# State space part by token tiles of 128: one decay matrix per head over both chunks of a tile

## The chip, the cores and the metric

The kernel runs on one core of a Trainium2 chip, in one launch. The metric is the device time of a run in microseconds; of the kernel before three runs are shown. The profile is of one more execution. Engines are named as in the profile: PE is TensorE's matmul, PEld its weight load, DVE is VectorE, ACT ScalarE, POOL GpSimd, SP SyncE, which issues the loads.

## The reference, cut to what matters

A first block (16 meta tokens and 256 tokens, width 1024) has a mixer of two branches, gated linear attention and a state space part, and then a retrieval feed-forward with 16384 experts; a second block has retention and stick-breaking attention. The change is in the state space part alone (32 heads of 64 columns in 4 groups of 8; state 128). The reference walks it in chunks of 64 tokens:

```python
def ssd_chunk_step(S, inp):
    xdt, a, Bc, Cc = inp
    acum = jnp.cumsum(a, axis=1)
    seg = jnp.exp(-jnp.abs(acum[:, :, None] - acum[:, None, :]))
    cb = jnp.einsum('btgn,bsgn->btsg', Cc, Bc)
    y = jnp.einsum('btsgr,btsg,bsgrp->btgrp', seg, cb, xdt)
    y = y + jnp.einsum('btgn,bgrpn,btgr->btgrp', Cc, S, jnp.exp(acum))
    to_end = jnp.exp(acum[:, -1:] - acum)
    S = S * jnp.exp(acum[:, -1])[..., None, None] + jnp.einsum('bsgn,bsgr,bsgrp->bgrpn', Bc, to_end, xdt)
    return S, y
```

Inside a chunk every token sees every other one, earlier and later, by `exp(-|difference of the sums|)`; across chunks it sees earlier ones only, through the state S. y then gets `d_skip * x`, is multiplied by silu(z), normed in groups of 512 and goes through `w_up_ssd`.

## The kernel before, in words

**Stream.** All weights come as 512 KB chunks ("units", loaded by SP into four buffers `raw`). `do_split` (L202) makes of each a high part on ACT (`whi`, L208) and a low part on DVE (`wlo`, L209), four units ahead of their use (`AHEAD`), and PE makes three passes per product (L247). `stream_T` (L256) takes a unit of 128 output columns over 1024 rows: 8 x 3 = 24 passes with 256 or 272 tokens moving. `stream_N` (L282) takes a unit of 512 columns over 256 rows: two halves of 6 passes with 512 columns moving.

**Side work.** Everything else is written as generators in the list `sides`. While `ring["steps"]` is 2, `side_step` (L232) runs one piece of the first generator in the middle of a unit and one at its end; a generator that ends uses up a step too. `until(key)` (L696) runs steps at once until a result has been issued. The order so made is each engine's program order: every engine takes its instructions in that order and waits at semaphores. ACT and DVE instructions other than the splits are chained one behind another.

**Order around the change.** 8 units for B and C (convolved by `conv`, L675, on ACT and DVE: L679, L681, L683, and the silu L673 one unit later), 16 units for gates, 16 units for x (four per group of heads), 8 units for the product of the attention branch (L845), 16 units of z (`stream_N`; `use_z` L854 with the product L860 and the square L861), then 16 units over the 2048 features of y. `first_side` (L727) turns B and calls `decays(0)` during the gates. `ssd_side(g)` (L736) is appended when the fourth x unit of group g is used; `conv_x` (L828) forces `xsg{g-2}`, the turned x of the group whose buffer it takes. `y_side(g)` (L872) is appended after z block g: `rstd` (L329, small DVE instructions around one square root on ACT), `diagonals` (L319, L321 and L322), some empty steps, then transposes of y by `turned` (L324, products at L306) and splits (L316, L317). `y_side(3)` has its first piece issued at the end of z, before what is left in `sides`.

**The state space part.** In the gate part (L494 to L525) the running sums of `a` are made per chunk by a scan with resets, exps of them, one decay factor per chunk and head broadcast through PE (`dec`), and the sums go to DRAM (`scr`). `load_bc(g)` (L810) fetches them back as 4 transfers of 128 KB, each row broadcast to 64 partitions. `decays(g)` (L701) makes M: C.B products of 64x64 into one bank (L711), two subtractions (L714), `min(m, -m)` (L718), exp (L719), two products with C.B out of PSUM (L722); M is [128 tokens, tile, head, 64 tokens]. `ssd_side` turns x and makes XD, the skip part of Y (`turn`, L751, L754) and XE (`to_end`, L760), makes the state of the 16 meta tokens (L772, L773), and then for each of two tiles and two chunks: eight products M x XD of 64x64 for the 8 heads, the state read C x S (512 columns moving), and but for the last chunk the update B x XE and `S = S*dec + update` (L790, L793). `next(ahead)` runs a piece of `decays(g + 1)` in between. After each tile Y takes in the bank (L797), then the state part (L799, L802). Buffers: `bank_free[4]` to `[6]` for y, state read and update; `bank_free[7]` for C.B.

An fp32 product (`mm`, L306; transposes L309) shows as two passes in the trace.

## Time and profile before

| | us |
|---|---|
| runs: median, lowest, highest | 1656.56, 1653.85, 1658.47 |
| the profiled execution | 1659.78 |
| its span, from first to last instruction | 1658.0 |
| PE, DVE, ACT busy in it | 1440.6, 1103.1, 700.5 |

### The profile page before, as it was taken

To read this page: it belongs to the slowest core of one execution; us is meant where nothing else is said; L and a number is where in the kernel's file an instruction comes from. 1 tells how busy PE (TensorE), PEld (TensorE's weight loads), DVE (VectorE), ACT (ScalarE), POOL (GpSimd) and SP (SyncE) were. 2 spreads that over 40 slices of the span, in tenths; PEclk is the share of its full clock that TensorE was granted. 3 is DMA by queue.
4 is the path that set the end of the run, shared out by engine and by line. 5 is a ranking of instruction groups with operands and counts; after the bars stand their busy time and mean duration, and the time that the engine had idled before them with its cause. 6 is when DMAs were issued, how large, how long until landed. Compare 5 with 4: busy or idle time off the path is not lost. (4 is left out here: it accounts for less than half of the span.)

```text
span 1658.0 us, 19318 instructions
## 1 busy us (share of the span) xinstructions
PE 1440.6 (87%) x6761; PEld 1007.9 (61%) x6761; DVE 1103.1 (67%) x2091; ACT 700.5 (42%) x1196; POOL 300.1 (18%) x260
## 2 busy tenths in 40 slices
PE   6999898999899699878777877877799999799987
PEld 6987696776798534333333333333288688788866
DVE  5765468786667868777777777675577466645554
ACT  5664465434545332222222222221354465666853
POOL 0000000000001356445435444433100000000000
PEclk9999999999999889898989899989899999899999
DMA  6452253243464999999999999999845456454432
GB/s 219 145 163 80 87 169 98 89 141 103 152 217 163 419 414 421 422 421 421 422 421 422 421 421 422 420 421 407 305 134 178 135 178 196 127 160 140 153 118 85
DMA packets 78000, 415.64 MB, mean 251 GB/s; under 512 B 9024, under 2 KB 9024, under 8 KB 44880
## 3 DMA queue, kind: packets, MB, share of 16 engines
q0 software_dynamic: 36864, 268.45, 39.1%
q1 hardware_dynamic: 41040, 145.96, 27.8%
q8 instruction: 54, 0.88, 0.2%
q14 instruction: 42, 0.34, 0.1%
HBM read 413.29 MB, written 1.08 MB: 250 GB/s over the span
## 5 line engine op out<-in xcount | busy, mean ns | idle before, releaser
L306 PE MATMUL ps<-AR 128*128 128x512 f32 (+7 forms) x1368 | 413.7, 450 | 111.9 <-ACT AR L1167 76.1
L209 DVE TENSOR_TENSOR wlo<-raw,whi 128x1024 fp32r<-128x1024 f32 x257 | 312.1, 1222 | 176.6 <-ACT whi L208 174.5
L306 PEld LDWEIGHTS ps<-AR 128*128 128x128 f32 (+3 forms) x1368 | 201.7, 185 | 303.8 <-issue 150.7
L208 ACT ACTIVATE whi<-raw 128x1024 fp32r<-128x1024 f32 x257 | 269.7, 1054 | 131.4 <-PE ps L247 116.5
L247 PE MATMUL ps<-XH,whi 128*128 128x256 f32 (+1 forms) x1032 | 306.1, 297 | 6.3 <-DVE XL L317 4.5
L306 PE MATMUL ps<-SLAB,AR 128*128 128x512 f32 x516 | 252.3, 645 | 59.6 <-ACT AR L1167 59.0
L247 PE MATMUL ps<-XL,whi 128*128 128x256 f32 (+1 forms) x1032 | 297.3, 288 | 0.0
L247 PE MATMUL ps<-XH,wlo 128*128 128x256 f32 (+1 forms) x1032 | 297.1, 288 | 0.0
L1132 POOL DMA_INDIRECT AR<-in_peer_uv,C x127 | 149.8, 1180 | 710.7 <-PE ps L247 528.4
L306 PEld LDWEIGHTS ps<-SLAB,AR 128*128 128x128 f32 x516 | 104.3, 207 | 205.9 <-issue 123.2
L247 PEld LDWEIGHTS ps<-XH,whi 128*128 128x128 f32 x1032 | 200.9, 195 | 26.2 <-issue 14.9
L247 PEld LDWEIGHTS ps<-XL,whi 128*128 128x128 f32 x1032 | 200.7, 194 | 0.1
L247 PEld LDWEIGHTS ps<-XH,wlo 128*128 128x128 f32 x1032 | 200.4, 194 | 0.0
L1141 DVE CUSTOM_DVE_ANT_0 SLAB<-SLAB,AR 128x1024 f32<-128x1024 f32 x129 | 156.6, 1222 | 64.2 <-DMA SLAB<-in_peer_uv,C 64.2
L247 PE MATMUL ps<-whi,XH 128*128 128x512 f32 x480 | 196.6, 409 | 0.0
L1141 DVE CUSTOM_DVE_ANT_0 AR<-AR 128x1024 f32<-128x1024 f32 x127 | 154.2, 1223 | 55.9 <-DMA AR<-in_peer_uv,C 55.8
L247 PE MATMUL ps<-whi,XL 128*128 128x512 f32 x480 | 188.2, 392 | 0.0
L247 PE MATMUL ps<-wlo,XH 128*128 128x512 f32 x480 | 188.0, 392 | 0.0
L1132 POOL DMA_INDIRECT SLAB<-in_peer_uv,C x129 | 150.1, 1164 | 169.8 <-PE ps L306 132.5
L1167 ACT ACTIVATE AR<-C 128x128 f32<-128x128 f32 x254 | 84.1, 392 | 186.6 <-DVE C L1155 156.3
L1150 ACT ACTIVATE C<-C,SM 128x4 f32<-128x4 f32 (+2 forms) x68 | 20.2, 297 | 293.7 <-DVE C L1141 293.4
L247 PEld LDWEIGHTS ps<-whi,XH 128*128 128x128 f32 x480 | 90.7, 189 | 23.3 <-issue 5.6
(228 smaller groups left out, 1175.0 us busy)
## 6 DMA issues: line engine op xcount, KB each, us to landing
raw<-in_stream SPq DMA_DIRECT2D x257, 512.0 KB
SLAB<-in_peer_uv,C POOLq DMA_INDIRECT x129, 27.5
AR<-scr SPq DMA_DIRECT2D x16, 128.0 KB, 3.9
AR<-in_rows SPq DMA_DIRECT2D x4, 512.0 KB, 4.7
AR<-in_peer_uv,C POOLq DMA_INDIRECT x127, 27.1
AR<-in_con SPq DMA_DIRECT2D x1, 1280.0 KB, 5.4
AR<-in_xin SPq DMA_DIRECT2D x2, 512.0 KB, 5.1
AR<-in_xin SPq DMA_DIRECT2D x1, 1024.0 KB, 5.8
```

What stands on the lines that cost most here:

```text
L208: a = A(lambda e: e.activation(h[:, :], r, ACT.Copy), loaded[i], free, chain=False)
L209: b = V(lambda e: e.tensor_tensor(l[:, :], r, h[:, :].bitcast(F32), ALU.subtract), a, loaded[i], free, chain=False)
L247: tok = PE(lambda e, s=s, m=m, n=n: e.matmul(out_ap, s, m, start=first and n == 0, stop=last and n == 2), *(after if n == 0 else ()), sign ...
L306: return PE(lambda e: e.matmul(out_ap, l, r, start=start, stop=stop, skip_group_check=onto), *after, signal=sig)
L1132: G(lambda e: e.indirect_dma_start(slots[j], None, peer_uv, bass.IndirectOffsetOnAxis(ap=col, axis=0)).then_inc(s, 16), idx_pt[m // 16], f ...
L1141: dot_pt[m] = V(lambda e: e.tensor_tensor_reduce(u, u, HN[:, i, :], 1.0, 0.0, ALU.mult, ALU.add, AV[:, i, at:at + 1]), uv_in[m], chain=False)
L1150: gelu_pt[ms[0]] = A(lambda e: e.activation(CC[:, i, c], AV[:, i, c], ACT.Gelu_apprx_tanh, scale=SM[:, 24 + i:25 + i]), dot_pt[ms[-1]])
L1167: a = A(lambda e: e.activation(d, ident, ACT.Copy, scale=CC[:, i, c]), c_ready, dg_free.get(m - 4), chain=False)
```

## The change

The running sums are taken over tiles of 128 tokens (resets at tokens 0, 16 and 144), with one decay factor, at the border between the two tiles; M becomes [128 tokens, tile, head, 128 tokens] and also carries the part from the first chunk of a tile to its second, with C.B copied by ACT to a masked SBUF tile CBM whose lower left quarter stays zero. The state is read twice per group and updated once. The pieces of `decays` go from 5 to 7, those of `ssd_side` from 16 to 15, and 13 for the last group (by the count of `yield`). DY moves, as M is twice as long.

```diff
...
@@ gate part
-            v = V(lambda e: e.tensor_tensor_scan(STK[W, :], C1[W, C_SCAN:C_SCAN + T], dx, 0.0, ALU.mult, ALU.add))
+            V(lambda e: e.memset(dq, 1.0))
+            for at in (0, 16, 144):
+                V(lambda e, at=at: e.memset(dq[:, at:at + 1], 0.0))
+            v = V(lambda e: e.tensor_tensor_scan(STK[W, :], dq, dx, 0.0, ALU.mult, ALU.add))
...
-            for c in range(4):
-                at = 16 + 64 * c + 63
-                v = V(lambda e, c=c, at=at: e.tensor_scalar(SM[W, 32 + 32 * c:64 + 32 * c], C1[W, C_ID:C_ID + 32],
-                                                            dq[:, at:at + 1], None, ALU.mult), c_ready)
+            v = V(lambda e: e.tensor_scalar(SM[W, 32:64], C1[W, C_ID:C_ID + 32], dq[:, 143:144], None, ALU.mult), c_ready)
-            tok = mm(ps[4][:, 0:128], SM[W, 160:288], SM[W, 32:160], True, True, True, v, v1, bank_free[4])
-            bank_free[4] = pts["dec"] = V(lambda e: e.tensor_copy(SM[:, 288:416], ps[4][:, 0:128]), tok)
+            tok = mm(ps[4][:, 0:32], SM[W, 160:288], SM[W, 32:64], True, True, True, v, v1, bank_free[4])
+            bank_free[4] = pts["dec"] = V(lambda e: e.tensor_copy(SM[:, 288:320], ps[4][:, 0:32]), tok)
...
@@ buffers
-        XE = place("XE", 18384, 1536).rearrange("p (i c) -> p i c", i=3)
-        M = place("M", 2768, 2048).rearrange("p (b i r t) -> p b i r t", b=2, i=2, r=8)
+        XE = place("XE", 18384, 1024).rearrange("p (i c) -> p i c", i=2)
+        CBM = place("CBM", 19408, 512).rearrange("p (b i t) -> p b i t", b=2, i=2)
+        M = place("M", 2768, 4096).rearrange("p (b i r t) -> p b i r t", b=2, i=2, r=8)
...
@@ decays(g)
             for i in range(2):
-                for c in range(2):
-                    cols = slice(16 + 128 * i + 64 * c, 16 + 128 * i + 64 * c + 64)
-                    tok = mm(ps[7][64 * c:64 * c + 64, 64 * i:64 * i + 64], BT[:, g, cols], CT[:, g, cols], True, True,
-                             i == 1 and c == 1, bank_free[7], [pts[f"c{f}"] for f in (16 + g, 20 + g)])
-            cb = tok
+                cols = slice(16 + 128 * i, 144 + 128 * i)
+                tok = mm(ps[7][:, 128 * i:128 * i + 128], BT[:, g, cols], CT[:, g, cols], True, True, i == 1, bank_free[7],
+                         [pts[f"c{f}"] for f in (16 + g, 20 + g)])
+            cbm = CBM[:, g % 2, :, :]
+            two = ps[7][:, 0:256].rearrange("p (i t) -> p i t", i=2)
+            A(lambda e: e.copy(cbm[0:64, :, :], two[0:64, :, :]), tok, cbm_zero, pts.get(f"M{g - 2}"))
+            cb = bank_free[7] = A(lambda e: e.copy(cbm[64:128, :, 64:128], two[64:128, :, 64:128]))
             for i in range(2):
                 v = V(lambda e, i=i: e.tensor_tensor(
-                    Mg[:, i, :, :], Mg[:, i, :, :], STN[:, i, 8 * g:8 * g + 8].unsqueeze(2).broadcast_to([128, 8, 64]),
+                    Mg[:, i, :, :], Mg[:, i, :, :], STN[:, i, 8 * g:8 * g + 8].unsqueeze(2).broadcast_to([128, 8, 128]),
                     ALU.subtract), pts[f"bc{g}"])
-            yield
-            v = V(lambda e: e.scalar_tensor_tensor(Mg, Mg, -1.0, Mg, ALU.mult, ALU.min))
-            a = A(lambda e: e.activation(Mg, Mg, ACT.Exp), v)
-            yield
+                yield
+            for i in range(2):
+                v = V(lambda e, i=i: e.scalar_tensor_tensor(Mg[:, i, :, :], Mg[:, i, :, :], -1.0, Mg[:, i, :, :], ALU.mult, ALU.min))
+                a = A(lambda e, i=i: e.activation(Mg[:, i, :, :], Mg[:, i, :, :], ACT.Exp), v)
+                yield
             for i in range(2):
...
+                    Mg[:, i, :, :], Mg[:, i, :, :], cbm[:, i, :].unsqueeze(1).broadcast_to([128, 8, 128]), ALU.mult), a, cb)
-            pts[f"M{g}"] = bank_free[7] = v
+            pts[f"M{g}"] = v
...
@@ first_side()
+            nonlocal cbm_zero
+            cbm_zero = V(lambda e: e.memset(CBM[:, :, :, :], 0.0), pts["ox"])
...
@@ ssd_side(g)
             to_end(0)
             yield
-            to_end(1)
-            yield
             for i in range(2):
-                for c in range(2):
-                    rows_ = slice(64 * c, 64 * c + 64)
...
+                cols = slice(16 + 128 * i, 144 + 128 * i)
+                tok = mm(ps[5][:, :], CT[:, g, cols], SS[:, :], True, True, True, s_ready, bank_free[5])
+                if i == 0:
+                    u = mm(ps[6][:, :], BN[:, 0, 128 * g:128 * g + 128], XE[:, 0, :], True, True, True, bank_free[6], xe[0])
+                    k = 288 + 8 * g
+                    V(lambda e: e.tensor_tensor(
+                        SS.rearrange("p (r c) -> p r c", r=8), SS.rearrange("p (r c) -> p r c", r=8),
+                        SM[:, k:k + 8].unsqueeze(2).broadcast_to([128, 8, 64]), ALU.mult), u, pts["dec"])
+                    s_ready = bank_free[6] = V(lambda e: e.tensor_tensor(SS[:, :], SS[:, :], ps[6][:, :], ALU.add))
+                for r in range(8):
+                    tok = mm(ps[4][:, 64 * r:64 * r + 64], Mg[:, i, r, :], XD[:, i, 64 * r:64 * r + 64], True, True, r == 7,
+                             m_ready, xd[i], bank_free[4])
+                pts["pe_ssd"] = tok
+                next(ahead, None)
+                yield
...
@@ load_bc(g)
+            for i in range(2):
+                src = scr[i, 8 * g:8 * g + 8, :].rearrange("r t -> (r t)").unsqueeze(0).broadcast_to([128, 1024])
+                pts[f"bc{g}"] = dma(SP, M[:, g % 2, i, :, :].rearrange("p r t -> p (r t)"), src, s_bc[g % 2], pts["scr"],
                                     pts["ox"], pts.get("pe_ssd"))
...
-        DY = place("DY", 4816, 512).rearrange("p (b i c) -> p b i c", b=2, i=2)
+        DY = place("DY", 0, 512).rearrange("p (b i c) -> p b i c", b=2, i=2)
...
```

## Rows read from the trace of the kernel before

**Rows 1.** The page: busy time of each engine; GB/s in 40 slices of the span.

```profile
PE 1440.6 (87%) x6761; PEld 1007.9 (61%) x6761; DVE 1103.1 (67%) x2091; ACT 700.5 (42%) x1196; POOL 300.1 (18%) x260
...
GB/s 219 145 163 80 87 169 98 89 141 103 152 217 163 419 414 421 422 421 421 422 421 422 421 421 422 420 421 407 305 134 178 135 178 196 127 160 140 153 118 85
```

**Rows 2.** By stretch: length, busy of PE, PEld, DVE, ACT, POOL; clock, DMA share, GB/s.

```profile
239.90:290.80 50.90, 43.29 (x308) 34.94 (x306) 42.81 (x63) 25.18 (x40) 0.00 (x0) 0.97 0.36 107
290.80:334.00 43.20, 41.97 (x292) 33.65 (x292) 32.15 (x46) 16.65 (x22) 0.00 (x0) 0.92 0.28 89
334.00:355.00 21.00, 20.08 (x144) 13.90 (x142) 18.05 (x26) 4.95 (x5) 0.00 (x0) 1.00 0.52 165
355.00:396.00 41.00, 40.87 (x213) 27.04 (x212) 31.14 (x38) 17.33 (x24) 0.00 (x0) 1.00 0.33 104
396.00:423.90 27.90, 26.11 (x134) 21.72 (x134) 18.48 (x35) 18.90 (x27) 0.00 (x0) 1.00 0.47 137
423.90:437.00 13.10, 8.42 (x56) 7.82 (x55) 8.02 (x23) 8.05 (x15) 0.00 (x0) 0.89 0.47 168
```

**Rows 3.** Timeline of PE, x stream: start, length, line, operands, passes, idle before.

```profile
251.45 0.29 PE L247 MATMUL ps<-XH,whi 128*128 128x272 f32 x1
251.58 0.29 PE L247 MATMUL ps<-XL,whi 128*128 128x272 f32 x1
...
254.19 3.20 PE L306 MATMUL ps<-AR 64*64 64x64 f32 x20
...
265.37 0.45 PE L306 MATMUL ps<-AR 128*64 128x64 f32 x8
...
267.45 1.14 PE L306 MATMUL ps<-AR 64*64 64x64 f32 x16
268.86 2.12 PE L306 MATMUL ps<-AR 128*64 128x512 f32 x4 [0.27 <-DVE AR L799]
...
272.63 2.21 PE L306 MATMUL ps<-AR 64*64 64x64 f32 x18
...
283.95 1.74 PE L309 MATMUL ps<-C,AR 128*128 128x128 f32 x12
```

**Rows 4.** Groups by line and shape, 200 to 560 us: count, busy us, mean ns, idle before.

```profile
L306 PEld LDWEIGHTS ps<-AR 64*64 64x64 f32 x256 | 16.1, 134 | 3.4 <-issue 1.4 <-DVE wlo L209 0.4 <-DVE AR L754 0.4
L306 PEld LDWEIGHTS ps<-AR 128*128 128x128 f32 x120 | 15.6, 197 | 8.7 <-DVE AR L322 6.8 <-ACT AR L1026 1.7
...
L790 DVE TENSOR_TENSOR AR<-AR,SM 128x512 f32<-128x512 f32 x12 | 8.3, 692 | 9.3 <-PE ps L306 8.8
...
L679 ACT COPY AR<-ps 128x272 f32<-128x272 f32 x16 | 6.2, 387 | 24.3 <-PE ps L247 23.6
...
L714 DVE TENSOR_TENSOR AR<-AR 128x512 f32<-128x512 f32 x8 | 5.5, 692 | 5.4 <-DMA AR<-scr 4.9
...
L718 DVE SCALAR_TENSOR_TENSOR AR<-AR 128x1024 f32<-128x1024 f32 x4 | 4.9, 1225 | 0.1
...
L719 ACT ACTIVATE AR<-AR 128x1024 f32<-128x1024 f32 x4 | 4.2, 1059 | 23.8 <-DVE AR L718 23.8
```

**Rows 5.** The transfers from scr, 205 to 360 us: issue ns, time to landing.

```profile
L188 SPq DMA_DIRECT2D AR<-scr x16: 451/596/937, 210.4 to 344.8; - x16
...
DMA to landing us min/median/max: 2.7/3.9/5.3
```

**Rows 6.** Waits, 239.9 to 290.8 us: us in total, times, longest.

```profile
DVE AR L683 <- ACT AR L681: 4.9, 4, 2.2
```

**Rows 7.** Timeline of PE behind the forced transposes.

```profile
290.78 2.07 PE L306 MATMUL ps<-AR 16*128 16x512 f32 x2 [5.10 <-DVE AR L760]
```

**Rows 8.** Timeline of PE where y is turned.

```profile
418.02 1.16 PE L306 MATMUL ps<-AR 128*128 128x128 f32 x8 [1.79 <-DVE AR L322]
...
433.79 1.77 PE L306 MATMUL ps<-AR 128*128 128x128 f32 x8 [4.33 <-DVE AR L322]
```

**Rows 9.** Timeline of DVE after the z stream.

```profile
430.24 0.29 DVE L322 TENSOR_SCALAR AR<-C,SM 128x128 f32<-128x128 f32 x1
```

More of the change, by code:

```diff
@@ L157, in build @@
         ps = [ctx.enter_context(nc.psum_tensor(f"ps{i}", [128, 512], F32)) for i in range(8)]
-        scr = nc.dram_tensor("scr", [4, 32, 64], F32).ap()
+        scr = nc.dram_tensor("scr", [2, 32, 128], F32).ap()
         PE = Engine(sem("s_pe"), False)
@@ L523, in gates_side @@
             s_scr = sem("s_scr")
-            pts["scr"] = dma(SP, scr.rearrange("c r t -> r c t"), STK[W, 16:T].rearrange("p (c t) -> p c t", c=4), s_scr,
+            pts["scr"] = dma(SP, scr.rearrange("i r t -> r i t"), STK[W, 16:T].rearrange("p (i t) -> p i t", i=2), s_scr,
                              pts["stk"])
@@ L664, in build @@
         xp_free = [None, None]
+        cbm_zero = None
         v0 = V(lambda e: e.memset(XP[:, :, 0:3], 0.0), x_ready)
@@ L759, in to_end @@
             def to_end(i):
-                xe[i] = V(lambda e: e.tensor_tensor(heads(XE[:, i, :]), heads(XD[:, i, :]), each(STN[:, i, 32 + 8 * g:40 + 8 * g]),
+                xe[i] = V(lambda e: e.tensor_tensor(heads(XE[:, i // 2, :]), heads(XD[:, i, :]), each(STN[:, i, 32 + 8 * g:40 + 8 * g]),
                                                     ALU.mult))
@@ L775, in ssd_side @@
             yield
-            to_end(1)
-            yield
             for i in range(2):
-                for c in range(2):
-                    rows_ = slice(64 * c, 64 * c + 64)
-                    cols = slice(16 + 128 * i + 64 * c, 16 + 128 * i + 64 * c + 64)
-                    for r in range(8):
-                        mm(ps[4][rows_, 64 * r:64 * r + 64], Mg[rows_, i, r, :], XD[rows_, i, 64 * r:64 * r + 64], True, True,
-                           False, m_ready, xd[i], bank_free[4])
-                    tok = mm(ps[5][rows_, :], CT[:, g, cols], SS[:, :], True, True, True, s_ready, bank_free[5])
-                    pts["pe_ssd"] = tok
-                    if not (i == 1 and c == 1):
-                        u = mm(ps[6][:, :], BN[rows_, i, 128 * g:128 * g + 128], XE[rows_, i, :], True, True, True, bank_free[6], xe[i])
-                        k = 288 + 32 * (2 * i + c) + 8 * g
-                        V(lambda e, k=k: e.tensor_tensor(
-                            SS.rearrange("p (r c) -> p r c", r=8), SS.rearrange("p (r c) -> p r c", r=8),
-                            SM[:, k:k + 8].unsqueeze(2).broadcast_to([128, 8, 64]), ALU.mult), u, pts["dec"])
-                        s_ready = bank_free[6] = V(lambda e: e.tensor_tensor(SS[:, :], SS[:, :], ps[6][:, :], ALU.add))
-                    next(ahead, None)
-                    yield
@@ L811, in load_bc @@
             until("ox")
-            for c in range(4):
-                i, rows_ = c // 2, slice(64 * (c % 2), 64 * (c % 2) + 64)
-                src = scr[c, 8 * g:8 * g + 8, :].rearrange("r t -> (r t)").unsqueeze(0).broadcast_to([64, 512])
-                pts[f"bc{g}"] = dma(SP, M[rows_, g % 2, i, :, :].rearrange("p r t -> p (r t)"), src, s_bc[g % 2], pts["scr"],
+            for i in range(2):
+                src = scr[i, 8 * g:8 * g + 8, :].rearrange("r t -> (r t)").unsqueeze(0).broadcast_to([128, 1024])
+                pts[f"bc{g}"] = dma(SP, M[:, g % 2, i, :, :].rearrange("p r t -> p (r t)"), src, s_bc[g % 2], pts["scr"],
                                     pts["ox"], pts.get("pe_ssd"))
```

10 lines of the change are left out of this document (4 added, 6 removed).

## The prediction

> **What bounds the kernel now.** The page comes first: one execution of 1658.0 us in which PE is busy 87%, DVE 67%, ACT 42% [rows 1]. Those are averages, so the view by stretches comes next, cut where the state space work begins and ends [rows 2]. From 239.9 to 423.9 us PE is busy in 172.3 of 184.1 us (43.29 + 41.97 + 20.08 + 40.87 + 26.11), DVE in 142.6. PE is the bound, but in the first stretch DVE has 42.8 of 50.9 us, 84%: take work from PE there and DVE is next. The timeline of PE then shows what the side work costs [rows 3], and the same view further on, with the groups of instructions by line, where PE stands and for whom.
>
> The order of everything is fixed by the program: two side steps per streamed unit (a unit is 24 passes; two starts in [rows 3], at 251.45 and 251.58, are 0.126 apart, so 3.03 us). I number steps by units of the 16 that make x: ssd_side(0) starts at 4.0; now it takes 16 steps per group (the last one only ends it), so the second is at 12.0 when the use of unit 12 forces three steps at 13.0. y_side(0) follows ssd_side(3) at 34.5, y_side(1) at 37.5, y_side(2) at 40.5; the z stream ends at 40.0.
>
> **PE work of a group, before.** A step for one chunk holds 16 passes 64x64 (8 products, two passes each), two passes of the state read and two of the update: 3.20 us, twice in this group, and once in two pieces, 1.14 + 2.12; the last chunk has no update, 2.21 [rows 3]. Sum 11.87 us, of which the modelled tails are about 0.2: 11.7. The C.B products are 8 short passes, 0.45 us [rows 3], and 4 full ones after: nothing.
>
> **After.** Two state reads and one update: 3 x 1.06 (2.12 for two products, [rows 3]) = 3.2 us; 64 or 128 contracted rows don't show in those times. The 16 passes of a tile now have 128x128 weights and still 64 moving columns, a form that no row has. Below: the 64x64 passes, 1.14 us for 16. Above: 12 transposes with 128x128 weights and 128 columns took 1.74 [rows 3], so 16 would take 2.3. The weight loads are nearest: 134 ns for 64 columns, 197 for 128, so 63 ns more per 64 columns [rows 4]; if loading bounds the pass it grows from 58 (1.14 less a 0.22 tail, by 16) to about 110 ns. I take 110 ns, 1.8 us per tile, and keep 1.14 and 2.3. Per group 3.2 + 3.6 = 6.8 against 11.7: 4.9 us saved, ends 3.9 and 6.2; four groups 19.6, ends 15.6 and 25.
>
> The Trainium skill (TensorE: Matmul & The Clock Gate, section LDWEIGHTS) gives a load P/1.2 ns for P columns whatever the rows, so 53 ns becomes 107 and the fewer, fuller products hardly gain in this part. The 63 ns per 64 columns agrees; by the page's figure the saving would be 5.1 us a group in place of 4.9.
>
> **DVE and ACT.** Durations from [rows 4]. Per group the decays cost DVE now 4 instructions of 512 elements (0.692) and one of 1024 (1.225) = 3.99; after, 6 of 1024: 7.35, so +3.36. Gone: one to_end (0.692) and two of three state updates (2 x 2 x 0.692): -3.46. Net -0.1: DVE does not get lighter. Its waits for the update products (8.8 us in 8, [rows 4]) shrink, since there is one update instead of three and it is issued ahead of the 16 passes. ACT gets one more exp (1.06) and two copies (0.39 for 272 columns, so at most 0.8): +1.9 on an engine that is half idle. No silu falls between the two exps of groups 1 to 3, so no table load (1.28) is added. The four memsets and three fewer tensor_scalars in the gate part, the 512-column memset of CBM and the narrower dec copy lie in the streams before 239.9 us, inside the four units by which splits lead: nothing, bounds -1 and +1 us.
>
> **DMA.** 4 x 128 KB become 2 x 512 KB per group; issue to landing is 3.9 us median, 5.3 worst [rows 5]. SP issues two where it issued four, behind the same wait for PE, with the raw loads queued behind them: not worse. The extra 512 KB at 422 GB/s, the most in a slice [rows 1], is 1.2 us, at half that 2.5. DVE waited for this transfer once, 4.9 us [rows 4], in the gate stream, where PE had no gap; it will be 6 to 8 us, inside the four units (12 us) that splits run ahead. The other groups give it three side steps (4.5 us or more) as now. What is queued behind the waiting subtraction is wlo, then PE. Cost nothing, worst +3.
>
> **Step counts.** After, an ssd_side takes 15 steps (the last group 13). Three consequences.
> (a) Stretch 239.9 to 290.8, up to the forced step: PE stands 5.10 us for L760 behind the forced transposes [rows 7]. PE saves 4.9 here, but DVE's own order up to that L760 is unchanged at 42.8 us of work; the 8.1 us it is idle are mostly the wait for ACT's L681 (4.9, [rows 6]) and small gaps. I let DVE reach 90% (42.8/0.9 = 47.5): gain 3.4 us, floor 0, ceiling 5.6 (DVE gapless but for 2.5 us). PE waits longer at 285.69, not less, and the half clock behind it stays (0.92 over 43.2 us in [rows 2], so 3.5 us lost).
> (b) 290.8 to 396: three groups, 14.7 us. DVE has 81.3 of 105.2 us; 81.3/90.5 is 90%, again at that edge. I take 13, floor 5.
> (c) 423.9 on: z ends with y_side(3) and then y_side(2) issuing their rstd; PE stands 4.33 us up to 433.79 for the second L322 [rows 8], and the clock of the stretch is 0.89 [rows 2], 1.4 us lost. After, y_side(0) starts at 32.0, (1) at 35.0, (2) at 38.0, so (2) has its diagonals ready two units before PE wants them, at 41.5. Gone: 4.3 + 1.4 = 5.7. Late next is y_side(3), whose diagonals end at 430.5 [rows 9], 6.6 us after the z stream (423.9), as now, and are wanted at 44.0, 12 us after: covered. On the other hand y_side(0) now starts right behind the square of its block, as (3) does: 6.6 us from the last z pass to L322, against three steps of 6 passes with 512 columns (0.126 x 512/272 x 6 = 1.4 us each, an estimate), 4.2 of cover: a gap of 2.4, where y_side(1)'s gap of 1.79 at 418.02 [rows 8] goes. With a chance of half-rate time behind it I count -1.
>
> Sum 3.4 + 13 + 5.7 - 1 = 21 us. The profiled execution took 1659.78 (1658.0 of span, 1.8 around it), 3.2 above the median 1656.56; against the median: 1635.5.
>
> **Rivals.**
> 1. VectorE is the bound throughout. For it: 84% and 86% (18.05 of 21.0) in two stretches, and the two engines meet at each group (PE waits for L799 at 268.86 in [rows 3], for L760 in [rows 7]). Against: 76% in 290.8 to 396 and 41 us of it at PE 100%. Then (b) gives its floor of 5 and (a) 1.5: with 5.7 - 1 that is 11, less 3.5 for one more spell of half rate like the one in (a): 8, so 1648.5.
> 2. The weights load free and the passes stay at 58 ns: 1.3 us a group more (5 in all), 1630.5. For it: loads run beside the passes in every stream (PEld 61% busy, PE 87%); against: the 12 transposes in 1.74.
> 3. The stall at the z end stays (the change does not shift it as I count, or DVE's order brings another wait): 6 less, 1641.5. For it: the diagonals come out of a chain of small instructions between DVE and ACT with splits in between [rows 9], where a new wait is easily made; against: three groups give half a unit each and one more.
> 4. Slower. One mechanism: each exp sits in ACT's queue until DVE has made its operand, and the whi splits queue behind it. Now 23.8 us in 4, 5.95 each [rows 4]. Two per group hold ACT 2 x (5.95 + 1.06) = 14.0 us, against the 12.1 us of lookahead; with the 5.1 us DVE is behind PE at the forced step, PE stands 14.0 - 12.1 + 5.1 = 7.0 us and pays 1.7 for half rate (half of the 3.5 above): 8.7 in each of groups 1 to 3, 26 in all, 5 above the gain: 1661. It decides from a hold of 12 us. Against it: the two exps are a step apart, the second's operand is made while the first waits, and in 355 to 396, which holds the last exp, PE is busy 40.87 of 41.0 us.
>
> **Chances.** Forecast 0.42; rival 1 0.22; rival 2 0.15; rival 3 0.14; rival 4 0.07. 0.3% is 5 us, what can be told from no change. Rival 1 leaves 0.03 within it and rival 4 0.01; slower 0.06, same 0.04, faster 0.90. Range 1624 (cheap passes, all of DVE's idle time used) to 1649 (rival 1).
>
> **What would show it.** The 64-column passes near 1.8 us for 16; L306 busy down by some 20 us; DVE above 88% in the x stretch, with a longer PE wait for to_end behind the forced transposes; no gap before the L306 transposes after the z stream; bc transfers landing within 6 us. Wrong if PE's gaps grow by as much as its work shrinks, or if DVE's sum in these stretches changes by more than 2 us.

## The result and the profile after

The changed kernel takes 1669.46 us (median of 7 runs, 1662.78 to 1675.78) against 1656.56 for the kernel before in the same comparison; ratio 1.0075, 95% interval 1.0052 to 1.0098. It is slower by 0.75%, some 13 us. The prediction said 1635.5, range 1624 to 1649, with 0.06 for slower: wrong in sign, by 34 us. The profiled execution of after is its slowest run, 1675.78 us (span 1673.9), so its trace shows more of the loss (15.9 us of span) than the median does.

The page after, busy time of each engine and the group of the side products (answers to [rows 1]):

```profile
PE 1430.0 (85%) x6585; PEld 1014.4 (61%) x6585; DVE 1102.3 (66%) x2077; ACT 703.3 (42%) x1206; POOL 300.4 (18%) x260
...
L306 PE MATMUL ps<-AR 128*128 128x512 f32 (+8 forms) x1192 | 398.0, 485 | 132.6 <-ACT AR L1168 79.8
```

PE did 10.6 us less, although more of it ran at half rate. DVE's sum moved by 0.8. So the work is as forecast; the time went elsewhere. By stretches, with the columns of [rows 2] (the borders are set by the waits of this trace and don't lie at the same work as there):

```profile
226.40:242.30 15.90, 12.38 (x97) 12.15 (x96) 13.45 (x18) 14.46 (x21) 0.00 (x0) 1.00 0.52 169
242.30:290.10 47.80, 41.17 (x260) 37.74 (x260) 33.73 (x48) 19.72 (x33) 0.00 (x0) 0.86 0.34 109
290.10:303.30 13.20, 0.04 (x1) 0.05 (x1) 10.41 (x14) 8.41 (x13) 0.00 (x0) 0.61 0.31 88
303.30:343.50 40.20, 37.85 (x236) 33.68 (x236) 27.53 (x37) 16.79 (x24) 0.00 (x0) 0.83 0.29 91
343.50:382.00 38.50, 33.55 (x188) 27.16 (x188) 30.06 (x37) 10.32 (x13) 0.00 (x0) 0.91 0.42 135
382.00:412.00 30.00, 23.70 (x81) 16.45 (x81) 18.63 (x23) 8.21 (x13) 0.00 (x0) 0.72 0.34 105
```

The third line is the picture of the case: 13.2 us in which PE does nothing and DVE is busy for 10.41. In [rows 7] the same wait was 5.10. The timeline of PE after, with the columns of [rows 3]:

```profile
259.22 2.86 PE L306 MATMUL ps<-AR 128*128 128x512 f32 x18 [0.52 <-DVE AR L766]
...
268.58 5.81 PE L306 MATMUL ps<-AR 128*128 128x512 f32 x22 [1.91 <-DVE AR L801]
...
303.25 2.07 PE L306 MATMUL ps<-AR 16*128 16x512 f32 x2 [13.18 <-DVE AR L766]
...
420.60 1.16 PE L306 MATMUL ps<-AR 128*128 128x128 f32 x8 [2.24 <-DVE AR L322]
```

(L766 is the `to_end` that was L760, L801 the emptying of bank 5 that was L799, L306 the product line of both.) The waits view of after, 205 to 425 us, shows who stood for whom: line, releaser, us in total, times, longest.

```profile
ACT AR L724 <- DVE AR L723: 26.5, 8, 5.8
...
PE ps L306 <- DVE AR L766: 22.2, 4, 13.2
...
ACT AR L715 <- PE ps L306: 16.7, 3, 6.8
DVE AR L685 <- ACT AR L683: 15.7, 6, 6.0
...
DVE AR L718 <- DMA AR<-scr: 6.0, 1, 6.0
...
PE ps L306 <- DVE AR L801: 4.7, 3, 2.3
...
PE ps L309 <- ACT AR L675: 4.2, 1, 4.2
...
PE ps L247 <- ACT AR L694: 3.5, 1, 3.5
```

The same view of the kernel before, PE alone:

```profile
PE ps L306 <- DVE AR L760: 6.0, 2, 5.1
PE ps L309 <- ACT AR L673: 2.2, 1, 2.2
PE ps L306 <- DVE AR L322: 1.8, 1, 1.8
PE ps L306 <- DVE AR L799: 0.9, 2, 0.6
```

To compare kernels I line them up by the low splits (L209, one per unit, the same work in the same order everywhere). "Split 44" is in the gates, 52 near the end of the gates, 64 near unit 12 of x, 84 in z, 100 behind z. Worked out from the traces, between the starts of splits 44 and 100:

```
                     wall   PE gaps  lost to half rate  the rest
before               261.5    17.6         8.5           235.4
after                276.6    41.4        25.0           210.2
start of split       52     64     84     96     100   (after less before, us)
                    +3.8  +12.5  +25.0  +15.4  +13.6

                            (a) split 52 to the meta-state  (b) from there   (c) split 84
                            product of group 1              to split 84      to 100
before                      62.5                            96.8             71.6
after                       71.1                           109.3             60.3
e3  read in bank 6          64.7                           100.5             61.2
e13 and 14 steps            60.8                            97.0             57.8
e14 as e8, 15 steps         62.3                           101.0             61.9
e10 before, less PE work    61.2                            89.4             70.3
```

(The last four kernels are told of below.) The borders hold the same units of the stream, but not the same side work: in before the last two chunks of group 3 (32 of the 64-column passes) come behind split 84, in after all of group 3 comes ahead of it. So (b) of after holds a little more side work, and (c) less.

"PE gaps" are idle times over 0.25 us (shorter ones count in "the rest"); "lost to half rate" is half of the time outside gaps in which the records show a granted clock of 1.2 GHz in place of 2.4. PE's work fell by 25.2 us, and gaps (+23.8) and half rate (+16.5) gave back 40. The experiments ask what made the gaps.

### The profile page after: what moved, and what is told of

It is laid out like the page before. It is cut to its first block and busy times, and to the rows that moved or that the text cites. A ratio compares the mean times of both kernels' runs of the same rounds, so it can differ in the third digit from the quotient of the medians.

```text
span 1673.9 us, 18970 instructions
## 1 busy us (share of the span) xinstructions
PE 1430.0 (85%) x6585; PEld 1014.4 (61%) x6585; DVE 1102.3 (66%) x2077; ACT 703.3 (42%) x1206; POOL 300.4 (18%) x260
## 5 line engine op out<-in xcount | busy, mean ns | idle before, releaser
L306 PE MATMUL ps<-AR 128*128 128x512 f32 (+8 forms) x1192 | 398.0, 485 | 132.6 <-ACT AR L1168 79.8
L209 DVE TENSOR_TENSOR wlo<-raw,whi 128x1024 fp32r<-128x1024 f32 x257 | 311.5, 1221 | 183.5 <-ACT whi L208 181.4
L306 PEld LDWEIGHTS ps<-AR 128*128 128x128 f32 (+4 forms) x1192 | 203.5, 205 | 317.2 <-issue 145.3
L247 PE MATMUL ps<-XH,whi 128*128 128x256 f32 (+1 forms) x1032 | 307.6, 298 | 9.7 <-DVE XL L317 5.1
L306 PE MATMUL ps<-SLAB,AR 128*128 128x512 f32 x516 | 253.3, 646 | 61.8 <-ACT AR L1168 61.0
L247 PE MATMUL ps<-XL,whi 128*128 128x256 f32 (+1 forms) x1032 | 299.1, 290 | 0.0
L247 PE MATMUL ps<-XH,wlo 128*128 128x256 f32 (+1 forms) x1032 | 298.9, 290 | 0.0
L306 PEld LDWEIGHTS ps<-SLAB,AR 128*128 128x128 f32 x516 | 104.0, 206 | 208.7 <-issue 122.6
L247 PEld LDWEIGHTS ps<-XH,whi 128*128 128x128 f32 x1032 | 202.8, 197 | 22.5 <-DVE XL L317 8.1
L247 PEld LDWEIGHTS ps<-XL,whi 128*128 128x128 f32 x1032 | 202.8, 196 | 0.1
L247 PEld LDWEIGHTS ps<-XH,wlo 128*128 128x128 f32 x1032 | 202.5, 196 | 0.0
L247 PE MATMUL ps<-whi,XH 128*128 128x512 f32 x480 | 197.2, 411 | 0.0
L247 PE MATMUL ps<-whi,XL 128*128 128x512 f32 x480 | 189.1, 394 | 0.0
L247 PE MATMUL ps<-wlo,XH 128*128 128x512 f32 x480 | 188.9, 394 | 0.0
L247 PEld LDWEIGHTS ps<-whi,XH 128*128 128x128 f32 x480 | 91.4, 190 | 19.8 <-issue 2.5
```

The lines of the kernel that those rows point to most:

```text
L209: b = V(lambda e: e.tensor_tensor(l[:, :], r, h[:, :].bitcast(F32), ALU.subtract), a, loaded[i], free, chain=False)
L247: tok = PE(lambda e, s=s, m=m, n=n: e.matmul(out_ap, s, m, start=first and n == 0, stop=last and n == 2), *(after if n == 0 else ()), sign ...
L306: return PE(lambda e: e.matmul(out_ap, l, r, start=start, stop=stop, skip_group_check=onto), *after, signal=sig)
```

## Experiments

All were compared over 5 rounds with the kernel before on the same chip (its medians 1656.2 to 1659.1), so ratios can be set side by side. 0.001 is 1.66 us. Stretches, gaps and waits are read from the one profiled execution of each.

### Is it ScalarE's new copies?

**e1_cb_late**: the changed kernel, the two copies of C.B behind the second exp.

```diff
-            A(lambda e: e.copy(cbm[0:64, :, :], two[0:64, :, :]), tok, ...)      # before the subtractions
-            cb = bank_free[7] = A(lambda e: e.copy(cbm[64:128, :, 64:128], ...))
+                if i == 1: (the same two, behind the exp of tile 1)
```

> The changed kernel, with the two ACT copies of C.B issued behind the second exp (two and a half side steps later); nothing else moved. Theory A (the copies hold ACT's queue for PE, 16.7 us in three groups, the x convolution behind them waits, and DVE idles 6.0 us in front of L685 for it): the wait in front of the copies falls below 2 us, DVE's idle in front of the convolution halves, the 13.2 us gap of PE behind the forced transposes falls to 6 to 8, and the time falls from 1669 to about 1657 (1652 to 1662). Theory B (DVE's pieces are too large and bunched, the copies only stand where ACT would wait for the convolution's input anyway): less than 4 us, 1665 to 1669.

Measured 1672.36, ratio 1.0100 [1.0083, 1.0118]: nothing won against after (1.0075 [1.0052, 1.0098]).

**e2_before_cbcopy**: the kernel before, with such copies added.

```diff
-            cb = tok
+            A(lambda e: e.copy(cbm[:, 0:64], ps[7][:, 0:64]), tok, ...)
+            cb = bank_free[7] = A(lambda e: e.copy(cbm[:, 64:128], ps[7][:, 64:128]))
```

> The kernel before, with C.B copied by ACT from PSUM to SBUF (two copies of 128x64 per group, at the place where the change has them) and the product taken from there. Theory A: ACT waits here for PE too, so some 5 to 10 us slower than before, 1662 to 1667, with DVE idle in front of the convolution. Theory B: within 2 us of before, 1655 to 1659.

Measured 1657.74, ratio 1.0012 [1.0002, 1.0022]. The copies cost next to nothing where they are added and nothing is won where they are moved: they are not the cause. The 6.8 us for which L715 waits in after is ACT waiting for PE, which itself waits.

### The second state read and bank 5

**e3_bank6**: the changed kernel; the state read of tile 1 goes to bank 6 (free by then), so that it doesn't wait until L801 has emptied bank 5.

```diff
-                tok = mm(ps[5][:, :], CT[:, g, cols], SS[:, :], ..., bank_free[5])
+                rb = 5 + i
+                tok = mm(ps[rb][:, :], CT[:, g, cols], SS[:, :], ..., bank_free[rb])
```

> The changed kernel, with the second state read of a group going to the bank of the update (free once the update is added, for which the read waits anyway) in place of the bank that L801 must empty. Theory C (the second tile is issued one step behind L801, so PE stands for DVE, 4.7 us in three, half clock follows, and what waits behind it, the copies of C.B on ACT above all, waits with it): the L801 waits vanish, C.B comes earlier and the time falls by 5 to 10 us, to 1660 to 1665. Theory A alone, or B: 1 to 3 us less, as PE waits for M or the drained y bank instead.

Measured 1658.04, ratio 1.0017 [1.0001, 1.0033]: 0.0058 less than after, 9.6 us. The same question from the other side:

**e7_extra_step**: the changed kernel, bank 5 kept, with one empty step between L801 and the second read.

```diff
                 pts[f"y{g}{i}"] = V(... yg, yg, IN ...)
                 next(ahead, None)
                 yield
+                if i == 0:
+                    yield
```

> The changed kernel (second read in the bank that L801 empties, as it was) with one more empty side step between L801 and the second read, so 16 steps per group again. If the short distance from L801 to the read is what cost 11 us (shown so far only by using another bank), the L801 waits shrink from 4.7 us in three to under 2 and the time falls by 6 to 10 us, to 1659 to 1663, though the z end loses its advantage of a step. If the other bank helped for another reason, 1667 or more.

Measured 1663.87, ratio 1.0049 [1.0035, 1.0064]: 0.0026 less than after, with intervals that overlap. The L801 waits shrink from 4.7 us in 3 to 1.2 in 2, and stretch (b) falls from 109.3 to 96.0 us, while (c) grows from 60.3 to 66.4, as more steps lie behind split 84. So it supports e3, in the stretch where the wait was, but as a whole it is not clear of noise. In after one tile's read, emptying and next read lie so close that the second read waits for L801, and in program order behind it stand the C.B products, behind these ACT's L715, behind this the conv copies and DVE's L685: the waits of L801, L715 and L685 above. That this chain is what makes 2 us into 10 is argued from the order; e1, where L715 stood elsewhere, shows that it is not needed in just this form (there PE waited 3.6 us for the exp in its place). In the kernel before more steps lay between, and the wait was 0.9 us in 2.

### What the step count does

**e4_before15**: the kernel before, `to_end(1)` in the step of `to_end(0)`: 15 steps instead of 16.

```diff
             to_end(0)
-            yield
             to_end(1)
```

> The kernel before, with the second to_end in the piece of the first, so that each group takes 15 side steps and not 16; the same instructions. By the prediction's step (c) y_side(2) has its diagonals ready before z ends: PE's 4.33 us wait for L322 and the half rate behind it go, 1656.6 falls to about 1651 (1649 to 1654), and no wait comes in x. Rival: fewer steps crowd DVE in the x stream and give the same back: 1655 to 1660.

Measured 1657.20, ratio 1.0023 [1.0002, 1.0044]. The stall of 4.33 us behind z [rows 8] is gone as forecast in (c), but 6.9 us of shift there had been built up before it by other waits and half rate: stretch (b) takes 106.0 us in place of 96.8, (c) 64.8 in place of 71.6, and nothing is won.

**e8_bank6_oneexp**: e3 with one min and one exp over both tiles, and so one step fewer, 14.

```diff
-            for i in range(2):
-                v = V(... Mg[:, i, :, :] ... ALU.min)
-                a = A(... Mg[:, i, :, :] ... Exp, v)
-                yield
+            v = V(... Mg ... ALU.min)
+            a = A(... Mg ... Exp, v)
+            yield
```

> The kernel with the second read in the update's bank, with one scalar_tensor_tensor and one exp over both tiles of M (2048 elements) in place of two each, in one step: the same elements, two instructions and one step less per group. If two exps per group in ACT's queue are what holds the convolution and the splits (rival 4 of the prediction), ACT's wait for DVE falls and the time by 3 to 6 us, to 1652 to 1655. If the holding is by the bunching of DVE's work, the longer pair holds ACT longer at a time: same or 1 to 4 us slower, 1657 to 1662.

Measured 1647.89, ratio 0.9950 [0.9930, 0.9970]: 11 us less than e3. Two things were changed at once, so they were then taken apart.

**e13_twoexp_14steps**: e3 with both min/exp pairs kept, but in one step.

```diff
                 a = A(lambda e, i=i: e.activation(Mg[:, i, :, :], Mg[:, i, :, :], ACT.Exp), v)
-                yield
+            yield
```

> The changed kernel with the second state read in bank 6 (1658.0 us, ratio 1.0017 with 15 steps per group), with both halves' min and exponential kept as two instructions each but issued in one step of work instead of two: 14 steps. The one-exponential kernel (0.9950) differed from it in both. If the step fewer made its 10 us: ratio 0.994 to 0.997. If the second exponential in ScalarE's queue made them: 1.000 to 1.003.

Measured 1646.45, ratio **0.9943 [0.9927, 0.9958]**.

**e14_oneexp_15steps**: e8 with an empty step behind the exp (`+ yield`).

> The one-exponential kernel (1647.9 us, 0.9950, 14 steps) with one empty step behind the exponential: 15 steps as in the changed kernel. The other half of the same question: if the step count is what counts, 1.000 to 1.003; if the number of exponentials is, 0.994 to 0.997.

Measured 1655.17, ratio 0.9992 [0.9978, 1.0005]. With 14 steps two exps are as good as one (0.9943, 0.9950); with 15 both lose 7 to 12 us. It is the step, not the second exp in ScalarE's queue (the two kernels with 15 steps are 4 us apart, with intervals that just overlap). (In the kernel before, one step fewer gained nothing, e4: what a step is worth belongs to the order around it.) Waits of PE, 200 to 430 us, in e13 and then in e14:

```profile
PE ps L306 <- DVE AR L766: 19.3, 5, 10.0
PE ps L309 <- ACT AR L675: 4.2, 1, 4.2
PE ps L247 <- ACT AR L694: 1.0, 1, 1.0
PE ps L306 <- DVE AR L322: 0.6, 1, 0.6
```

```profile
PE ps L306 <- DVE AR L766: 21.3, 4, 11.7
PE ps L309 <- ACT AR L675: 3.9, 1, 3.9
PE ps L306 <- ACT AR L779: 3.2, 1, 3.2
PE ps L306 <- DVE AR L322: 2.3, 1, 2.3
```

The step more shows only late: at split 64 the two kernels are level (+1.5 and +1.8 against before), at 84 they stand at +0.6 and +6.0, at 96 at -11.6 and -2.0. It brings back a wait for the copy of the meta state in the last group, one for y's diagonals, and 2 us of the wait for `to_end`.

**e17_after_14steps**: the changed kernel with that one `yield` removed and bank 5 kept.

> The changed kernel with nothing altered but the yield between the two min/exponential pairs: both pairs in one step of work, 14 steps per group instead of 15; the second state read still waits in bank 5. With that read in bank 6 the same edit was worth 0.0074 (1.0017 to 0.9943). If the two losses (the read's wait, the 15th step) are separate, they add up: ratio 0.999 to 1.002. If they are one loss seen twice: 1.005 or above (nothing left to win here), or 0.996 and below (the step alone takes both away).

Measured 1660.30, ratio 1.0017 [1.0005, 1.0029]: 0.0058 less than after. The two losses add up: 0.0075 - 0.0058 (bank) - 0.0058 (step) = 0.9959 would be the plain sum, 0.9943 was measured for both.

**e18_twoexp_13steps**: e13 with the two subtractions in one step as well (one `yield` fewer again).

> The second state read in bank 6, both min/exponential pairs in one step (1646.5 us, 0.9943 with 14 steps) and both subtractions of the decays in one step too, as in the kernel before: 13 steps. If each step less goes on paying: 0.988 to 0.991. If 14 steps already bring the groups in ahead of the gated stream and what is left is VectorE's backlog at the forced transposes: 0.993 to 0.996, with the 10 us gap in its place.

Measured 1652.19, ratio 0.9969 [0.9951, 0.9987]: 4 us worse than 14 steps, with intervals that just overlap; e16 below, also with 13 steps, points the same way. Stretch (a) gets shorter still (59.0 us), (b) longer (104.0 against 97.0). Fewer steps are not always better. Its longest wait for `to_end` is 8.3 instead of 10.0 us, but L766 takes 20.4 us in 6 in place of 19.3 in 5.

**e5_bank6_spread0**: e3 with two empty steps in `decays(0)` only, for the 3.5 us that PE waits in the gates (L247 for L694: a bank held by a sigmoid queued behind the exps).

> The kernel with the second read in the update's bank (1658.0), and in the decays of group 0 alone two more empty steps between the transfers of the sums and the first subtraction. Theory D (in the gate stream DVE stands 6 us for the larger transfer, the six wide instructions and two exps bunch behind it, and the sigmoids behind the second exp in ACT's queue hold a bank that PE wants: 3.8 us, then 2.7 behind it in front of the first transposes): both waits shrink to under 1 us, DVE's wait for the transfer to under 2, and the time falls by 4 to 6 us, to 1652 to 1654. Rival: the same work lands two steps later on the x convolution and PE waits there: 1656 to 1660.

Measured 1658.19, ratio 1.0011 [0.9998, 1.0025], e3 had 1.0017. The 3.8 us gap in the gates went, and the next one, ahead of the transposes, grew from 2.7 to 5.9 us.

### VectorE's share

**e6_bank6_halfm**: e3 with M's subtraction, min, exp and product done for heads 0 to 3 of each group only; heads 4 to 7 use M as loaded.

```diff
-                    Mg[:, i, :, :], Mg[:, i, :, :], STN[:, i, 8 * g:8 * g + 8]...broadcast_to([128, 8, 128]),
+                    Mg[:, i, 0:4, :], Mg[:, i, 0:4, :], STN[:, i, 8 * g:8 * g + 4]...broadcast_to([128, 4, 128]),
```

> The kernel with the second read in the update's bank, with subtraction, min, exp and product of M done for heads 0 to 3 of each group only; the other half of M is used as it was loaded. DVE loses 3.7 us and ACT 1.06 per group, PE nothing, step counts stay. If VectorE's work is what takes the place of PE's (rival 1 of the prediction), the 13.2 us gap behind the forced transposes falls by the 3.7 to 5 us and the time by 10 to 16 us, to 1642 to 1648. If it is the order of waits between ACT, DVE and PE, and not the amount, 2 to 6 us: 1652 to 1656.

Measured 1647.31, ratio 0.9946 [0.9930, 0.9962]: 12 us less than e3 for 14.7 us less of DVE work (half of 24 instructions of 1.225 us); ScalarE's exps are halved with it, some 4 us, so the two are not told apart. The wait behind the forced transposes falls from 13.2 to 9.7 us. By stretches (a) falls from 64.7 to 62.3 us, (b) from 100.5 to 93.4: in the changed kernel less VectorE work is worth most in (b).

**e15_oneexp_pool**: e8 with the eight subtractions on GpSimd.

```diff
-                v = V(lambda e, i=i: e.tensor_tensor(Mg[:, i, :, :], ..., ALU.subtract), pts[f"bc{g}"])
+                gs = G(lambda e, i=i: e.tensor_tensor(Mg[:, i, :, :], ..., ALU.subtract), pts[f"bc{g}"], V.now())
```

> The one-exponential kernel with the eight 128x1024 subtractions of the decays (1.22 us each on VectorE) on GpSimd, which does nothing else in this stretch. Theory (what TensorE still waits for is VectorE's backlog: 47.9 us of work between split 52 and split 64, 56.7 us of wall time, the same in five kernels with 46 to 54 us of TensorE work): that stretch falls below 54, the 10.6 us gap below 6, ratio 0.989 to 0.993. Rival (the exponential then waits for the slower subtraction, or the two engines hinder each other): 0.995 or above.

Measured 1651.67, ratio 0.9975 [0.9965, 0.9986]: 4 us worse than e8 (0.9950 [0.9930, 0.9970]), at the edge of noise. Timeline of GpSimd and VectorE in e15 (start, length, line, operands, count, idle before):

```profile
274.48 1.90 POOL L718 TENSOR_TENSOR AR<-AR 128x1024 f32<-128x1024 f32 x1 [4.95 <-DVE AR L804]
274.51 3.25 DVE L685 SCALAR_TENSOR_TENSOR AR<-AR,PAR 128x272 f32<-128x272 f32 x3
...
312.14 1.90 POOL L718 TENSOR_TENSOR AR<-AR 128x1024 f32<-128x1024 f32 x1 [35.76 <-DVE AR L685]
312.23 2.90 DVE L209 TENSOR_TENSOR wlo<-raw,whi 128x1024 fp32r<-128x1024 f32 x1 [0.22 <-ACT whi L208]
...
319.39 1.23 DVE L209 TENSOR_TENSOR wlo<-raw,whi 128x1024 fp32r<-128x1024 f32 x1
319.47 2.90 POOL L718 TENSOR_TENSOR AR<-AR 128x1024 f32<-128x1024 f32 x1 [5.43 <-DVE AR L804]
```

Three L685 that take 1.57 us elsewhere take 3.25, a split that takes 1.22 takes 2.90, each while GpSimd's 1.90 us instruction runs; where VectorE was first, GpSimd's took 2.90. In these rows the two take turns, so the offload saves VectorE less than it seems, and the min then waits 8.5 us in all for the slower subtraction. The Trainium skill (SBUF — State Buffer, section SBUF: two separate sides) calls the port pair of the two an exclusive lock held for a whole instruction; these rows agree.

**e16_oneexp_ahead**: e8 with the next group's decays moved on in six steps instead of four (`next(ahead, None)` once more per tile).

> The one-exponential kernel, with the next group's decays moved on in each of the six last steps of a group instead of in four of them, so that they are spread as in the kernel before. If the bunching of the decays' instructions right ahead of the forced transposes makes the 10.6 us gap: it falls below 7 and the ratio to 0.990 to 0.993. If the sum of VectorE's work up to there decides: the gap stays within 2 us, ratio 0.994 to 0.997.

Measured 1654.57, ratio 0.9990 [0.9978, 1.0001]. The longest gap fell from 10.6 to 8.4 us and others grew; the sum of gaps is the same (29.6 against 28.8 us). It does more than that: the piece of the decays that stood alone at the end of a group is gone, so a group has 13 steps, not 14. (b) takes 105.1 us, as in e18 with 13 steps (104.0), against 96.5 in e8. Whether spreading helps is therefore not shown.

**e11_inter_later**: e8 with the meta-state product one step later.

```diff
             yield
+            to_end(0)
+            yield
             tok = mm(ps[6][:, :], BN[0:16, 2, ...], XE[0:16, 1, :], ...)
             s_ready = bank_free[6] = A(...)
-            to_end(0)
             yield
```

> The one-exponential kernel with the second state read in bank 6 (1647.9 us, 0.9950), with the meta-state product two... one step later than now: to_end(0) alone in the step after the forced transposes, then the meta-state product and its copy, then the first read; 15 steps instead of 14. Theory (the product stands in TensorE's queue right behind the forced transposes while VectorE is 10 us behind, so the stream products behind it wait too): the gap of 10.6 us at split 64 falls below 6, ratio 0.990 to 0.993. Rival (VectorE's backlog must be worked off by the stream's own splits anyway, so the wait only moves to the next product that needs a low split): the gap goes, others of the same sum come, ratio 0.994 to 0.997.

Measured 1658.38, ratio 1.0000 [0.9984, 1.0016], no better than e14, which has the same 15 steps: the gap at the meta-state product stayed at 10.5 us. The theory that the product's place makes it falls.

### TensorE's share: work and rate

**e10_before_lesspe**: the kernel before, without two of the three update products and two of the four state reads of each group; all else stays.

```diff
+                    if c == 0:
                         tok = mm(ps[5][rows_, :], CT[:, g, cols], SS[:, :], ...)
-                        u = mm(ps[6][:, :], BN[rows_, i, ...], XE[rows_, i, :], ...)
+                        if i == 0 and c == 0: u = mm(...)      (else u = tok)
```

> The kernel before, with only TensorE's work cut: two of the three 64-row state update products and two of the four state reads of a group are left out (4 of about 1.06 us, 4.2 us per group, 17 in four), every VectorE, ScalarE and DMA instruction stays, in the same 16 steps. My prediction's reading (TensorE sets the time of these stretches but for what VectorE holds back): 10 to 16 us less, ratio 0.991 to 0.994. Rival (VectorE's order sets it already, TensorE's savings turn into waits): within 4 us of the kernel before, ratio 0.998 to 1.000, and TensorE's gaps from split 44 to split 100 grow from 17.6 to 27 us or more.

Measured 1649.15, ratio 0.9936 [0.9914, 0.9957]: 10.6 us for 16.8 us of PE work (the rest column 218.6 against 235.4), gaps 21.4 against 17.6. In the kernel before, TensorE's work is worth 6 parts in 10. "TensorE's saving is worth nothing" falls for the order of the kernel before: in (b) 10.2 us less work make it 7.4 us shorter, where the prediction counted 13 for 14.7. In (a) nothing can be told: 61.2 us against 62.5, and e2, where no work was taken from PE, has 61.0.

**e9_filler**: the changed kernel, with 10, 3 and 2 products of no use ahead of the meta-state product of groups 1 to 3.

```diff
+            for _ in range((0, 10, 3, 2)[g]):
+                mm(ps[6][:, :], BN[:, 0, 0:128], BN[:, 0, :], True, True, False, bank_free[6], pts["bn"])
             tok = mm(ps[6][:, :], BN[0:16, 2, ...], XE[0:16, 1, :], ...)
```

> The changed kernel with 10, 3 and 2 extra TensorE products of 128x512 (1.06 us each at full clock, results overwritten) queued right ahead of the meta-state product of groups 1, 2 and 3, where TensorE stands 13.2 us and then some 4 us waiting for VectorE. They need nothing that VectorE still has to do. Theory (a part of the loss is TensorE at half rate behind long waits: 25.0 us lost from split 44 to split 100 against 8.5 before): the spell of 17.1 us from 293.0 shrinks to at most one short one, 5 to 10 us less in that stretch, ratio to the kernel before 1.001 to 1.004. Rival (the order of VectorE's work is the whole loss and half rate only fills time that would be waited anyway): 1.006 to 1.009 as now. If the extra products run at half rate themselves they last past VectorE and cost up to 8 us: ratio above 1.010.

**e12_oneexp_filler**: the same in e8.

> The one-exponential kernel with the second state read in bank 6 (1647.9 us, 0.9950), with the same extra products as the filler run: 10, 3 and 2 products of 128x512 ahead of the meta-state product of groups 1, 2 and 3. If half rate behind the 10.6 us gap (11.9 us lost from split 44 to 100) is worth something: 3 to 6 us less, ratio 0.991 to 0.993. If not: 0.995 or, where the extra products outlast the wait, up to 0.999.

Measured e9 1675.74, ratio 1.0096 [1.0067, 1.0124]; e12 1648.69, ratio 0.9945 [0.9923, 0.9967]. Timeline of PE in e9:

```profile
288.03 8.75 PE L306 MATMUL ps<-AR 128*128 128x512 f32 x20
301.38 2.07 PE L306 MATMUL ps<-AR 16*128 16x512 f32 x2 [4.61 <-DVE AR L766]
```

The wait of 13.18 us is down to 4.61, and the time does not fall; in e12 the sum of gaps drops from 28.8 to 17.1 us and the ratio is that of e8. So PE has some 13 us to spare in those waits. On half rate the two runs say little. The spell of 17.1 us in after begins at 293.0, inside the wait (290.07 to 303.25), and only 6.9 us of it lie behind the wait; in e9 the spell behind the wait lasts from 301.1 to 307.9, 6.5 us behind it. From split 44 to 100 the time lost to half rate falls only from 25.0 to 23.1 us (e12: 11.9 to 10.2). What the 16.5 us of more half rate in my table cost is open: the fillers did not take them away.

## Why the prediction was wrong

**PE's work: right in mechanism, low in size.** The passes with 128x128 weights and 64 columns start 111 to 112 ns apart (the 18 passes from 259.22 us), where I took 110; where the granted clock was 1.2 GHz, 213 to 214. L306 is 15.7 us less busy on the page, half-rate time included; by the table 25.2 us of work went in place of 19.6, the upper end I gave. Where the 5.6 us come from, at the price forecast for the passes, is not shown. The Trainium skill's rule (TensorE: Matmul & The Clock Gate, section LDWEIGHTS) gives 107 ns for 128 columns; this trace, at 111 to 112, is within 5% of it.

**DVE's sum: right.** 189.2 us between splits 44 and 100 against 189.4; -0.1 per group was forecast.

**DMA: right.** The transfers of 512 KB land after 5.2 us median, DVE's one wait grew from 4.9 to 6.0 us (6 to 8 forecast).

**The gate part, costed at nothing: wrong, +5.3 us.** Shift -1.5 at split 48, +3.8 at 52: both exps and the sigmoids share ScalarE's queue, and one sigmoid held a bank of the gate stream (3.46 us). e5 shows that filling this gap alone moves it.

**Step (a), "gain 3.4", failed.** The stretch took 71.1 us in place of 62.5. Without the wait in bank 5 it is 64.7 (e3), with 14 steps besides 60.8 (e13). I let DVE go from 84 to 90% busy; in e13 it is busy 52.2 of 60.8 us, 86%, which it was before too (53.5 of 62.5). Here PE's saving turns into waiting: 5.10 us behind the forced transposes became 13.18, and 9.98 in e13.

```profile
291.19 2.07 PE L306 MATMUL ps<-AR 16*128 16x512 f32 x2 [9.98 <-DVE AR L766]
```

(e13, timeline of PE.) What sets the 61 us is not settled. Fillers (e12, 61.2) don't move them, less DVE work at 15 steps (e6, 62.3 against 64.7) by 2.4, 13 steps (e18) to 59.0; and the kernel before itself takes 62.5 or 61.0 (e2), so 1.5 us are noise.

**Step (b), "gain 13", failed by 25 us: this is the term that decided.** The stretch took 96.8 us before and 109.3 after. Two causes, neither priced in my sum, account for the half of it that made the kernel slower. First, the second read of the state waits for bank 5: 9.6 us by the medians (e3 against after). In the profiled executions it is 8.8 us in (b) with 15 steps (109.3 to 100.5) and 9.1 with 14 (106.1 in e17 to 97.0 in e13), and 6.4 and 4.5 in (a); that of after is its slowest run, so its stretches add up to more than the medians do. e7 points the same way. I named the queues behind the DMA and the exps, but for the closeness that is new, read, emptying and read within a tile's three steps, I took the wait of 0.27 us in [rows 3] as if distances stayed. Second, the count of steps: I counted 16 to 15 as a gain at the z end only, and never asked what two steps of decays, each with its subtraction, and then two more for the exps do to where a group's pieces fall against the units. One step less is worth 9.6 us (e17) to 12 us (e13 against e3) over the whole kernel, and 3.2 to 4.5 us in (b) of the profiled executions; one less again costs some 4 us (e18).

With both put right (b) takes 97.0 us, level with before. The other half, the gain of 13 itself, never came. The stretches (b) of before and of e13 in the windows view, with the columns of [rows 2]:

```profile
290.80:387.60 96.80, 94.65 (x596) 69.92 (x597) 74.84 (x102) 35.33 (x44) 0.00 (x0) 0.96 0.36 114
```

```profile
291.20:388.20 97.00, 88.22 (x508) 72.63 (x509) 78.59 (x105) 38.46 (x53) 0.00 (x0) 0.89 0.38 122
```

PE's work there fell by 12.5 us (91.2 to 78.7, gaps and half rate taken out), near the forecast; gaps grew by 6.6 us and half rate by 6.1 and took it all back. The step that failed is the one from 14.7 us of PE work to 13 us of time: it needed DVE at 90% of a shorter stretch, and DVE never got there (81% in e13, 70% in after). What holds DVE and PE below that is not shown. Less DVE and ACT work shortens (b) by 7.1 us (e6).

**Step (c), "gain 4.7", right and more.** The stall of 4.33 us is gone and y_side(0)'s is 2.24 us (2.4 forecast). From split 84 to 100 the time falls by 11.3 us. 2.8 of it lie before split 92, where after has less side work left than before. From split 92, at the end of z, on it is 8.5 us (38.4 to 29.9), and 7.6 to 8.6 in every other kernel with 15 or fewer steps, e4 among them: it comes with the step count and is no catching up: e6 has 8.5 too, and it was ahead of the kernel before at split 84 already. Gaps fall by 3.7 us there, half rate by 1.7 and the rest by 3.2, which I had not counted.

**Rivals.** Rival 4 came out nearest (1661) and its mechanism is not what happened: ACT waits 26.5 us in 8 for its exps' operand where it waited 23.8 in 4, not 14 us per group, and one exp in place of two is worth nothing at equal steps (0.9950 and 0.9943 with 14; 0.9992 and 1.0017 with 15, where up to 4 us may be left). Rival 1 (1648.5) is 21 us off, but e6, where 14.7 us less of DVE work and 4 of ACT's are worth 12, and e12, where 13.4 us more of PE work in the waits cost nothing, speak for its mechanism in the changed kernel. But DVE is busy only 86% of (a) and 81% of (b) in the best version, so its sum alone is not the bound. The sum that I called sure, PE's, was indeed there; what I gave 0.10 to (slower 0.06, same 0.04), that its pieces would land worse among the others, decided.

**Best version.** e13, the changed kernel with the second read in bank 6 and both exps in one step: 1646.45 us, 0.9943 [0.9927, 0.9958], faster than both. That is 10 us of the 21 forecast. From split 44 to 100 its PE work is 25.7 us less than before; gaps take back 9.5 (27.1 against 17.6) and half rate 4.4 (12.9 against 8.5).

## What to carry to other kernels

When side work is dealt out in fixed steps between units of a stream, a change in the number or content of the steps moves every later piece, and one step was worth 10 us here, as much as the best version gained in all. Before counting a saving on the bound engine, list each buffer whose write and next write come closer, with the engine that must empty it between, and what stands behind the waiting instruction. And try the change at one step more and one fewer before judging it.

## What the runs showed of the hardware

The granted clock fell to 1.2 GHz around the long idle times of PE: before, at 290.8 us, as the wait of 5.10 us ended, for 6.8 us; after, at 293.0, 2.9 us into the wait of 13.18 us, for 17.1 us, of which 6.9 lie behind the wait. Passes with 128x128 weights and 64 columns start 111 to 112 ns apart at 2.4 GHz and 213 to 214 at 1.2. GpSimd and VectorE took turns for whole instructions where both worked in SBUF (1.22 us became 2.90).
